# Summing the older FFN blocks ahead of the last block, a fourth ordinary gate/up pair, and adaLN loads at other places

## The reference

```
mod = silu(c) @ w_ada + b_ada
sh1, sc1, g1, sh2, sc2, g2 = split(mod, 6)
h = rms_norm(x, g_pre_mix) * (1 + sc1) + sh1
x = x + g1 * rms_norm(mixers(h) @ w_out, g_post_mix)
h2 = rms_norm(x, g_pre_ffn) * (1 + sc2) + sh2
gate, up = split(h2 @ w_ffn_in, 2)
f = (silu(gate) * up) @ w_ffn_out
x = x + g2 * rms_norm(f, g_post_ffn)
```

## Time and profile before

| | |
|---|---|
| median of 3 runs | 2091.14 us (2090.91 to 2091.93) |
| the profiled execution | 2092.62 us, span 2090.8 us |
| PE busy | 2037.2 us, 97% of the span, 16217 matmuls |
| PEld, DVE, ACT, POOL busy | 94%, 49%, 30%, 51% |
| DMA | 211.93 MB, mean 101 GB/s |
| TensorE's clock, mean | 0.992 of full |

### The profile page before, as it was taken

One profiled execution on the slowest core, in us unless ns is written; L12 is line 12 of the kernel. 1 busy time (PEld: TensorE's weight loads), 2 busy tenths in 40 slices (PEclk: granted clock), 3 DMA queues, 4 the chain that ended last, 5 costly groups with the idle time before them and its releaser, 6 DMA issues. The chain is left out here.

```text
span 2090.8 us, 38528 instructions
## 1 busy us (share of the span) xinstructions
PE 2037.2 (97%) x16217; PEld 1964.2 (94%) x16217; DVE 1033.2 (49%) x1665; ACT 624.4 (30%) x1364; POOL 1058.4 (51%) x560
## 2 busy tenths in 40 slices
PE   8999999999999999999889999999999999999997
PEld 7999898999998999999879989989999999999997
DVE  5223466431348544638584335563223593647474
ACT  4111224110135342415332121340102354525252
POOL 0444454658762544453554544545687536354543
PEclk9999999999999999999999999999999999999999
DMA  9746221223351434343421262212232413223332
GB/s 361 251 132 61 67 76 51 74 82 91 86 177 30 159 104 145 103 157 93 167 72 41 74 65 72 65 52 84 71 101 81 162 33 100 82 82 90 93 92 76
DMA packets 299835, 211.93 MB, mean 101 GB/s; under 512 B 13792, under 2 KB 293904, under 8 KB 296464
## 3 DMA queue, kind: packets, MB, share of 16 engines
q1 hardware_dynamic: 292912, 205.94, 34.0%
q10 hardware_dynamic: 6752, 3.53, 0.8%
HBM read 204.65 MB, written 4.07 MB: 100 GB/s over the span
## 5 line engine op out<-in xcount | busy, mean ns | idle before, releaser
L946 PE MATMUL ps<-h_hi,hi_lo 128*128 128x288 f32 x3008 | 541.3, 298 | 0.3 <-POOL hi_lo L860 0.3
L857 POOL TENSOR_TENSOR hi_lo<-raw,consts 128x1024 fp32r<-128x1024 f32 (+1 forms) x124 | 237.7, 1917 | 468.9 <-PE ps L946 358.2
L946 PEld LDWEIGHTS ps<-h_hi,hi_lo 128*128 128x128 f32 x3008 | 446.6, 189 | 7.6 <-issue 5.3
L946 PE MATMUL ps<-h_lo,hi_lo 128*128 128x288 f32 x1504 | 322.4, 296 | 0.0
L873 POOL TENSOR_TENSOR a_lo<-raw,a_hi 128x512 fp32r<-128x512 f32 x114 | 169.7, 1489 | 274.3 <-ACT a_hi L2098 274.3
L860 POOL TENSOR_TENSOR hi_lo<-raw,hi_lo 128x1024 fp32r<-128x1024 f32 (+1 forms) x124 | 301.0, 2427 | 9.7
L946 PEld LDWEIGHTS ps<-h_lo,hi_lo 128*128 128x128 f32 x1504 | 242.8, 189 | 0.0
L973 PE MATMUL ps<-yf_hi,fo_l 128*128 128x288 f32 x704 | 151.8, 297 | 8.7 <-POOL fo_l L888 7.6
L973 PE MATMUL ps<-yf_hi,fo_h 128*128 128x288 f32 x704 | 153.3, 299 | 1.6 <-DVE yf_lo L2264 1.6
L1859 ACT ACTIVATE tmp<-ps 128x576 f32<-128x576 f32 x60 | 39.0, 651 | 380.7 <-PE ps L946 380.7
L973 PE MATMUL ps<-yf_lo,fo_h 128*128 128x288 f32 x704 | 151.3, 297 | 0.0
(11 more groups left out here) (398 smaller groups left out, 4602.0 us busy)
## 6 DMA issues: line engine op xcount, KB each, us to landing
raw<-in_w_in SPq DMA_DIRECT2D x108, 512.0 KB, 3.8
ada<-in_w_ada SPq DMA_DIRECT2D x23, 2048.0 KB, 9.2
raw<-in_w_ffn_in SPq DMA_DIRECT2D x152, 256.0 KB, 3.1
raw<-in_w_ffn_out SPq DMA_DIRECT2D x32, 384.0 KB, 3.4
raw<-in_w_ffn_out SPq DMA_DIRECT2D x32, 320.0 KB, 3.2
raw<-in_w_out SPq DMA_DIRECT2D x16, 512.0 KB, 3.9
raw<-in_w_ffn_in SPq DMA_DIRECT2D x12, 512.0 KB, 4.0
raw<-in_w_br_mlstm SPq DMA_DIRECT2D x8, 512.0 KB, 3.4
```

The costliest lines, as they stand in the source:

```text
L857: pool.tensor_tensor(hi, RAW[s][:, 0:size], ONES[:, 0:1].to_broadcast([128, size]), ALU.mult).then_inc(chunk_hi, 1)
L946: m = pe.matmul(o[:, h, :], a[:, k, c0:c0 + 128], mv(k, h), start=(k == 0 and begins), stop=(k == nk - 1 and a is wl))
```

## The change

The last block's output groups no longer start from zero. ACT copies the sum of the older blocks out of `OMID` into the group's PSUM unit (`preset`), and the matmuls accumulate onto it (`start` is false in the last block). PE waits for `o_preset` instead of the empty unit. `preset(0)` and `preset(1)` stand in ACT's list around the end of the last seven-product pair, `preset(k + 2)` behind the squares of tile k. DVE's `whole_tile` is gone; in layer 0 the products with `x` are made straight from PSUM in three pieces, in place, and added (`post_products`), and `products` and `new_squares` are summed by PE in and right behind `fo3_7`.

`PLAINP` is 4: four ordinary pairs in the first block, two seven-product pairs. Chunks `fi0_4` to `fi0_7` have their weights in slots 2 and 3 in turn.

Layer 1's parts 4 to 7 are computed in layer 1's q/k stage (at `qk4`, `qk5`, `wvif`, `qk6`) and parts 2 and 3 at `fo0_1` and `fo1_1` of layer 0; the loads of parts 2 and 3 are issued right behind the weight blocks of the second pair of their block. Part 8 is loaded behind chunk `fo3_5`'s weights, and parts 9 and 4 and the two tables behind `fo3_7`'s.

In `h_hi` of the FFN the whole copy of tile k is made after the high part of tile k + 1. In layer 1's last block the token transposes always use one unit and all other results take turns in the other three.

```diff
-NB, PLAINP = len(BLOCKS), 3
+NB, PLAINP = len(BLOCKS), 4
...
-ADA_IN.update({(1, a): 0 if a < 9 else 1 for a in range(HALVES)})
+ADA_IN.update({(1, a): 0 if a in (0, 1, 2, 3, 8) else 1 for a in range(HALVES)})
...
-             "fo0_1": (1, (2,), (0, 1)), "fo0_4": (1, (3,), (2,)), "fo1_1": (1, (4,), (3,)), "fo1_4": (1, (5,), (4,)),
-             "fo2_1": (1, (6,), (5,)), "fo2_4": (1, (7,), (6,)), "fo3_0": (1, (), (7,))},
-         1: {"qk4": (1, (), (8, 9)), "fo0_4": (1, (), (10, 11))}}
+             "fo0_1": (1, (2,), (0, 1)), "fo1_1": (1, (3,), (2,)), "fo2_1": (1, (), (3,))},
+         1: {"qk4": (1, (4,), (8, 9)), "qk5": (1, (5,), (4,)), "wvif": (1, (6,), (5,)), "qk6": (1, (7,), (6,)),
+             "wk": (1, (), (7,)), "fo0_4": (1, (), (10, 11))}}
...
+def unit_turns():
+    unit, turn, turns = {}, {}, [0] * UNITS
+    first = G[1, f"fo{NB - 1}_0"]
+    ring, others = first % UNITS, 0
+    for i, (l, n) in enumerate(ORDER):
+        u = i % UNITS
+        if l == 1 and i >= first:
+            u = (ring + 3) % UNITS if n[:2] == "gk" else (ring + others % 3) % UNITS
+            others += n[:2] != "gk"
...
-FIXED = {P_FFN + 5: 3}
+FIXED = {P_FFN + i: 2 + i % 2 for i in range(4, 2 * PLAINP)}
...
+                if l == 1:
+                    sp.wait_ge(chunk_used, done(1, "qk1"))
+                    part_load(sp, 1, 5)
                 for i, nm in enumerate(("qk6", "qk7", "wk")):
+                    if l == 1 and i < 2:
+                        ada_after(1, 6 + i, 4 + i)
...
+                        if r == 1:
+                            for a in AFTER[l].get(f"fo{c}_1", NOTHING)[1]:
+                                ada_after(1, a, a - 1)
                     for i in range(8):
-                        if (l, c, i) == (0, LASTB, 3):
-                            sp.wait_ge(s_prod, 7 * NSP)
-                            for a in IN_P2[1]:
-                                part_load(sp, 1, a)
...
+                        if (l, c) == (0, LASTB) and i in (5, 7):
+                            sp.wait_ge(s_prod, 7 * NSP)
+                            part_load(sp, 1, IN_P2[1][i == 7])
+                            if i == 7:
+                                part_load(sp, 1, 4)
...
                             for h in range(2):
-                                m = pe.matmul(o[:, h, :], a[:, k * 128:(k + 1) * 128], mv(k, h),
-                                              start=(k == 0 and begins), stop=(k == nb - 1 and a is wl))
+                                m = pe.matmul(o[:, h, :], a[:, k * 128:(k + 1) * 128], mv(k, h), skip_group_check=c == LASTB,
+                                              start=(k == 0 and begins and c < LASTB), stop=(k == nb - 1 and a is wl))
...
+                def preset(k):
+                    nm, older = f"fo{LASTB}_{k}", f"fo{LASTB - 1}_{k}"
+                    act.wait_ge(unit_of(l, nm), empty(l, nm))
+                    act.wait_ge(unit_of(l, older), read(l, older))
+                    act.activation(halves(l, nm), split2(OMID[:, k, :]), ACT.Copy).then_inc(o_preset, 1)
...
                 for k in range(8):
                     post_tile("p2", k)
+                    if k + 2 < 8:
+                        preset(k + 2)
...
+                def post_products(k):
+                    nm, sq, j = f"fo{LASTB}_{k}", f"p2q{k}", 8 + k
+                    held, o, g = 1 <= k < 7, halves(l, nm), SC[:, 3, k, :]
+                    if held:
+                        dve.wait_ge(osq_ready, nth(osq_ready, l, j))
+                        tt(split2(ACC[:, 0, :]), halves(l, sq), split2(ACC[:, 0, :]), ALU.add).then_inc(acc1_added, 1)
+                    dve.wait_ge(go_ready, nth(go_ready, l, j))
+                    for a, b, i, j2 in ((0, HALF, 0, 0), (HALF, SEQ, 1, 0), (SEQ, T, 1, 1)):
+                        x = o[:, i, a - i * HALF:b - i * HALF]
+                        m = dve.scalar_tensor_tensor(ACC[:, 1, a:b] if k == 0 else TS[:, 1, a:b] if k == 7 else x, x, g[:, j2:j2 + 1],
+                                                     X[:, k, a:b], ALU.mult, ALU.mult)
...
+                    dve.wait_ge(prod_ready, nth(prod_ready, l, k - 1))
+                    tt(split2(ACC[:, 1, :]), o, split2(ACC[:, 1, :]), ALU.add).then_inc(unit_of(l, nm), 1)
+                    dve.wait_ge(gsq_ready, nth(gsq_ready, l, j))
+                    dve.wait_ge(acc1_added, nth(acc1_added, l, 5 + k))
                     tt(split2(ACC[:, 2, :]), halves(l, sq), split2(ACC[:, 2, :]), ALU.add).then_inc(unit_of(l, sq), 1)
```

More of the change, by code:

```diff
@@ L206 @@
 UNITS = 4
+def unit_turns():
[7 more added lines that the diff above has]
+            others += n[:2] != "gk"
+        unit[l, n], turn[l, n] = u, turns[u]
+        turns[u] += 1
+    return unit, turn
+UNIT, TURN = unit_turns()
 P_QK, P_WVIF, P_WK, P_V, P_MO, P_WQ, P_SU, P_SV, P_BR = 0, 6, 9, 10, 14, 18, 22, 26, 30
@@ L1656, in _ @@
                 run_begins("fi0_4", P_FFN + 4)
-                feature_group("fi0_4", P_FFN + 4, 8, 128, 0, *HM, lead=True)
-                feature_group("fi0_5", P_FFN + 5, 8, 128, 0, *HM, lead=True, ahead=False)
+                for i in range(4, 2 * PLAINP):
+                    feature_group(f"fi0_{i}", P_FFN + i, 8, 128, 0, *HM, lead=True, ahead=i + 1 < 2 * PLAINP)
                 product_begins(0, 0, "p1")
@@ L1756, in post_tile @@
                     o = halves(l, nm)
[L1757 to L1760 removed]
+                    act.wait_ge(done_by(nm), done(l, nm))
                     if held:
@@ L1786, in h_hi @@
                            .then_inc(hh_ready, 1)
[L1787 to L1790 removed]
+                        if first and k:
+                            h_whole(k - 1, part)
                         if k == 0 and (l, first) != (0, 0):
@@ L1794, in h_hi @@
                             modulation_tile(lm, b)
+                    if first:
+                        h_whole(7, part)
                 def modulation_tile(lm, a):
@@ L2152, in _ @@
                 block_high("a12", 0, 0)
-                gate_tile(2)
+                for i in range(2, PLAINP):
+                    gate_tile(i)
+                    if i + 1 < PLAINP:
+                        high_y(i)
                 sum_high(1, 0, 0)
@@ L3005, in _ @@
                 low_y(1)
+                for i in range(2, PLAINP - 1):
+                    gated(i)
+                    low_y(i)
                 weight_sum(1, 0, 0)
```

137 lines of the change are left out of this document (58 added, 79 removed).

## The result

The changed kernel takes 2067.18 us (2065.50 to 2068.67, 4 runs), beside 2091.02 us (2087.95 to 2091.93, 4 runs) of the kernel before on the same chip: a ratio of 0.9888, 95% interval 0.9871 to 0.9905, or 23.8 us less. The forecast was 2064.6, in a range of 2060.0 to 2073.5.

The account below looks back on a forecast made before the run. PE was taken as the bound, busy 2037 of 2090.8 us, its idle time and half clock to be won; -3.5 - 2.4 - 12.1 - 7.1 - 0.8 - 0.8 - 0.5 + 0.7 = -26.5 gave 2064.6 us, range 2060.0 to 2073.5.

Parts of the forecast that it names:

- Step 1: Fourth ordinary pair in each layer: 3.2 us more PE work, but waits for `s_lo` and layer 1's half clock go; -3.5 us.
- The 0.9 "issue": Layer 0, right behind the wait for `s_lo`: a PE wait of 0.9 us put down to issue, expected to go.
- Step 2: Fewer adaLN loads between layer 0's output chunks: waits for `fo_l`, `c` and `tmp` go, 1.2 comes back; -2.4 us.
- step 5: Smaller ones: whole copies of `h_hi` -0.8, end of layer 1 -0.8, parts 4 to 7 in layer 1's q/k stage -0.5 us.
- the reserve: Allowance of +0.7 us kept in the sum, as the clock may fall once somewhere else.
- Step 3: Layer 0's last block, `fo3_0` to the end of `fo3_7`: 53.2 us becomes 41.1, -12.1 us.
- rival B: The preset loop binds: slower DVE pieces or ACT copy make each of six tiles wait 1 us; 2069 to 2072 us, chance 0.10.
- Step 4: From the end of `fo3_7` to layer 1's stream: 19.7 us becomes 12.2, +0.4 for the fifth chunk; -7.1 us.
- A: Data late elsewhere: 4.9 MB ahead of layer 1's first chunks make the stream wait 5 to 8 us; 2070 to 2075, chance 0.12.
- C: The first seven-product pair still waits, DVE or POOL being behind in the longer chain; 2068 to 2071 us, chance 0.12.
- D: Layer 0's last block: the wait moves to `fo3_6`, behind part 8, with 5 us left; 2070 us, chance 0.05.
- E: Slower: the `preset` hand-over stalls in both layers' last blocks, or half clock runs through both; about 2100 us, chance 0.015.

## Why the prediction was right, and where it was not

The sign, the size and the range held: 23.8 us of the median, 26.5 forecast. By its steps, against the profiled execution and its repetition:

*Step 1, the fourth pair*: -3.5 forecast, -3.6 measured, and +3.6 with three pairs again. The chain had room, as counted; the 0.2 for `fi0_6` was 0.29. The split into terms was less right: I gave layer 1 alone a stretch of half clock, and layer 0 has one too in both kernels with three pairs that ran later. The 0.9 "issue" that I took off in layer 0 was in neither, and a kernel with four pairs has one of 0.84, so it was no part of the change. With the half clock that usually stands there instead, the row came to the same.

*Step 2 and the moved parts of step 5*: -2.9 together, measured -3.5 and -2.0. The waits for `c`, `tmp` and `fo_l` went; `yf_lo` came in layer 0 with 0.79 and 0.73 (0.7 forecast). The difference of 1.5 between the executions is the half clock in layer 1's q/k stage, which the text had as a bound and the reserve as 0.7; that stretch was there in ten of twelve. New half clock in that stage was one of the signs that the prediction named of being wrong. It came, in all but two executions, and cost 1.5 us.

*Step 3, the last block*: -12.1 forecast and -12.1 measured. Nothing waited for a preset: the copy of tile 4 ends at 1015.98, and PE's last two matmuls of the group ahead, which wait for it, start at 1016.12.

```profile
1015.32 0.66 ACT L1785 ACTIVATE ps<-mid 128x576 f32<-128x576 f32 x1 [1.25 <-DVE acc L2314]
```

```profile
1016.12 0.50 PE L1000 MATMUL ps<-yf_hi,fo_l 128*128 128x288 f32 x2
```

So rival B was 0.14 us per tile away, and the prediction's "behind the wait stand only those two matmuls" was the wrong comfort: they end the group, and the ring closes over them.

*Step 4, to the stream*: -7.1 forecast, -3.2 and -1.3 measured with the stream. Up to the stream's first matmul alone it is -5.9 and -7.5, near the forecast; what is missing is lost in the stream, which is 2.7 and 6.2 us longer and for which the sum had no change. This is the step that was wrong, in one term: "The fifth lies beside the boundary's DVE work: +0.4 for the shared time". When the fourth chunk would be ready was about right (2.7 us ahead of the stream, 2 to 6 forecast), with two errors that nearly cancel: the first split began 34.9 us behind `fo3_0`, 5.6 later than forecast, and each then took 4.3 us, the lower end of 4.3 to 5.2. The price was taken as a share of a mild case, 0.76 against 1.30. It is a lock: what an operation pays is what is left of POOL's, 0.8 to 2.2 us a time in the profiled execution (less 0.13), and the mean of 1.84 for `tmp<-mid,x_resident` had hinted at that. In the stream's first two tiles PE waits for these operations one after the other, with nothing to hide them, and the clock falls behind. Against the 39.3 us without contention the term is 4.3 to 6.8 us, not 0.4. The Trainium skill has the rule, on a page that the prediction did not use ("SBUF — State Buffer", section "Who interferes with whom"): the port pair that DVE and GpSimd share is held for a whole instruction, and whoever issues second stands still. The traces agree: 0.61 to 0.62 us from the end of POOL's operation to the end of DVE's, 20 times in 20 among the boundary's additions.

*Step 5, the rest*: the order of the whole copies was put at 0.4 per layer and gave 0.86; the end of layer 1 -0.8, measured -0.9 (3.54 to 2.65 us behind the last group).

Why the total came out near in spite of step 4, which gave 3.9 less than forecast in the profiled execution: the copies gave 0.9 more, step 2 with the moved parts 0.6, layer 1's blocks 0.6 and its end 0.1, the reserve of 0.7 was not used, and the start was 1.4 us shorter in code that the change does not touch. Most of that is luck. The start scatters from 565.2 to 568.9 us over the kernels, and the number of half-clock stretches in its first 40 us, none to two, does not order it (568.3 with none, 566.0 with two); layer 1's blocks scatter by 1.2. The two medians of the changed kernel are 2.6 and 4.4 us above the forecast.

Of the rivals, A, C, D and E did not occur, and B only where two more copies were added. A was near the truth in its object, the 4.9 MB ahead of layer 1's chunks, and wrong in its mechanism: they did not make the stream wait for data, they pushed POOL's work into DVE's most exposed microseconds.

## What to carry to other kernels

When a change takes time out of one stage, ask which engine's background work will now lie beside the next stage's exposed chain, and price each meeting with the rest of the other engine's instruction, not with a share. Order loads by when their consumer's work should be over, not by when it is first needed: 2 MB moved behind five chunks took 3.5 to 5.4 us off boundary and stream here. To see 1 us in a kernel that scatters by 4, compare the lengths of stages between first instructions. And a slack that is read from a trace holds for one chain only; an engine in order adds up everything it does per tile.

## What the runs showed of the hardware

- A DVE addition of two SBUF operands, 128x576 fp32, takes 0.75 us alone. Started during an operation of POOL it ends 0.61 to 0.62 us behind that operation's end, in all of 20 cases at the boundary in ten executions, with lengths of 0.94 to 2.88; over the whole span it is so 59 to 70 times in each of the fourteen traces, with 0.61 to 0.63. Where an operand is read from PSUM, such an operation takes 0.74 to 0.77 beside POOL too. It goes both ways: POOL's subtraction took 2.81 instead of 2.36 where DVE was first by 0.18 and had 0.58 us left, so here too all but 0.13 us of the other's rest is paid. Who is first can change with the same code, and boundary and stream took 43.6 to 46.1 us.
- Half clock comes without any wait: over 1144 to 1146 us PE was busy throughout, and the granted clock was 0.54, behind 23 matmuls of one or four columns; two executions of twelve, one of them of the same kernel, did without. Behind a wait of 2.2 us for `s_lo` it came five times in six; the sixth ran the same code as one of the five.
- With token transposes taking turns in the PSUM units into which ACT copies sums, two outputs came out wrong by 0.32 and 0.36, at 42.85 us for the block as without; that the transposes are the cause was not tested.
